# A second convolution tile moved to VectorE while the projections run, and its diagonals loaded from DRAM

## The reference

```
z = h @ w_in                      # 1024 -> 22 tiles of 128 columns
cv_v, cv_g, lr_x, lr_y, q, k, v, g_lr, og = split(z)
u = cv_v * sigmoid(cv_g)
u = causal_dw_conv(u, conv_dw_w, conv_dw_b)    # 31 taps, 256 channels
u = silu(layer_norm(u, conv_ln_g, conv_ln_b))
r = rg_lru(causal_dw_conv(lr_x, ...), ...) * gelu(lr_y)
o = rms_norm(gla_chunked(q, k, v, lg), gla_norm_g) * silu(og)
mixed = concatenate([u, r, o]);  return mixed @ w_out
```

## Time and profile before

| | us |
|---|---|
| median of 3 runs | 2758.78 (2758.22 to 2760.03) |
| profiled execution, its own time | 2758.25 |
| span of the profiled execution | 2756.4 |
| TensorE busy | 2672.3 (97%) |
| VectorE busy | 1997.5 (72%) |
| ScalarE busy | 1463.9 (53%) |
| GpSimd busy | 190.8 (7%) |

### The profile page before, as it was taken

How to read it: one execution, slowest core, us unless ns; L and a number is a source line. 1 busy time by engine, 2 the same in 40 slices (tenths; PEclk the granted TensorE clock), 3 DMA queues, 4 the chain that set the end, 5 groups by cost and what they waited for, 6 DMA issues and landing times.

```text
span 2756.4 us, 46105 instructions
## 1 busy us (share of the span) xinstructions
PE 2672.3 (97%) x15974; PEld 2315.9 (84%) x15974; DVE 1997.5 (72%) x2965; ACT 1463.9 (53%) x2276; POOL 190.8 (7%) x70
## 2 busy tenths in 40 slices
PE   5999899999999989999999999999999999999999
PEld 3866778887999867788899987999877888899987
DVE  7855699998997556743899847998465753699954
ACT  3353589986554246742655525555246753555532
POOL 1431133330000000000000000000000000000000
PEclk9999899999999999999999999999999999999999
DMA  7740599992322231123233232232232123223222
GB/s 288 280 137 32 204 344 412 412 391 100 102 100 92 99 145 62 50 80 109 93 105 107 92 107 92 94 106 92 99 131 83 53 69 115 100 93 107 91 100 99
DMA packets 95470, 376.63 MB, mean 137 GB/s; under 512 B 10800, under 2 KB 11072, under 8 KB 93120
## 3 DMA queue, kind: packets, MB, share of 16 engines
q1 hardware_dynamic: 89584, 348.69, 35.3%
q0 software_dynamic: 4320, 15.73, 1.4%
q10 hardware_dynamic: 1456, 10.74, 1.0%
HBM read 363.59 MB, written 15.73 MB: 138 GB/s over the span
## 4 chain that ended last, share of the span: by engine, by line
PE 84%; DVE 6%; issue 4%; ACT 4%; DMA 1%; POOL 0%; ACTq 0%; DVEq 0%; SPq 0%; POOLq 0%
PE pb L1442 15%; PE pb L1443 15%; PE pb L1444 15%; PE pb L1887 10%; PE pb L1888 10%; PE pb L1889 10%; PE pb L2071 1%; PE pb L2103 1%; PE pb L2027 1%; PE pb L1521 1%; ACT SP L1324 1%; DVE hid L2818 1%; PE pb L1726 1%; PE pb L2080 1%; DVE SP L2970 0%
## 5 line engine op out<-in xcount | busy, mean ns | idle before, releaser
L1887 PE MATMUL pb<-bl,g_wh 128*128 128x256 f32 x2464 | 702.1, 285 | 11.0 <-DVE bl L2729 6.9
L1888 PE MATMUL pb<-bh,g_wl 128*128 128x256 f32 x2464 | 698.3, 283 | 0.0
L1889 PE MATMUL pb<-bh,g_wh 128*128 128x256 f32 x2464 | 698.2, 283 | 0.0
L1887 PEld LDWEIGHTS pb<-bl,g_wh 128*128 128x128 f32 x2464 | 473.6, 192 | 15.9 <-issue 9.7
L1888 PEld LDWEIGHTS pb<-bh,g_wl 128*128 128x128 f32 x2464 | 473.7, 192 | 1.6 <-issue 1.4
L1889 PEld LDWEIGHTS pb<-bh,g_wh 128*128 128x128 f32 x2464 | 473.7, 192 | 0.0
L2768 DVE TENSOR_TENSOR w_lo<-raw,w_hi 128x1024 fp32r<-128x1024 f32 x164 | 200.3, 1222 | 202.0 <-ACT w_hi L694 201.2
L1442 PE MATMUL pb<-hl,w_hi 128*128 128x512 f32 x720 | 299.9, 416 | 20.6 <-DVE hl L2231 9.9
L694 ACT ACTIVATE w_hi<-raw 128x1024 fp32r<-128x1024 f32 x194 | 204.3, 1057 | 187.9 <-PE pb L1444 174.0
L1443 PE MATMUL pb<-hh,w_lo 128*128 128x512 f32 x720 | 283.3, 393 | 0.0
L1444 PE MATMUL pb<-hh,w_hi 128*128 128x512 f32 x720 | 283.2, 393 | 0.0
(11 more groups left out here) (476 smaller groups left out, 5456.2 us busy)
## 6 DMA issues: line engine op xcount, KB each, us to landing
raw<-in_wstream SPq DMA_DIRECT2D x220, 512.0 KB, 3.3
m_raw<-in_moe_stream SPq DMA_DIRECT2D x96, 512.0 KB, 8.3
g_own<-in_gu_stream SPq DMA_DIRECT2D x44, 768.0 KB, 4.1
raw<-in_gu_stream SPq DMA_DIRECT2D x44, 768.0 KB, 4.2
m_first<-in_moe_stream SPq DMA_DIRECT2D x48, 512.0 KB, 6.7
hf<-in_moe_stream SPq DMA_DIRECT2D x48, 512.0 KB, 6.4
ada_ring<-in_ada SPq DMA_DIRECT2D x8, 2048.0 KB
g_own<-in_gu_stream SPq DMA_DIRECT2D x44, 256.0 KB, 3.1
```

Of the source, the lines that this page charges most:

```text
L1887: pe.matmul(o, lh, rl, start=first and k == 0, stop=False, skip_group_check=True)
L1888: pe.matmul(o, ll, rh, start=False, stop=False, skip_group_check=True)
L1889: m = pe.matmul(o, lh, rh, start=False, stop=k == 3, skip_group_check=True)
```

## The change

- Tile 1 has 5 taps on TensorE instead of 13. The other 26 are on VectorE, and they stand before `route_add`, in groups of 3, 6, 5, 6 and 6.
- Between these groups VectorE makes the low halves of chunks 18 to 21, which GpSimd made.
- GpSimd no longer builds diagonals. They come from a new DRAM input `conv_diag`, 36 matrices of 128x128, with one transfer on SyncE's queue after the loads of pairs 8 and 9, when VectorE is done with `ada_ring`, whose memory they take.
- TensorE does the 5 taps and the identity matmul before the heads, in one go. No taps stand between heads. The two ones matmuls stand before `head_rms(3)`.
- ScalarE's `conv_evac(1)` stands before the first head's square.

```diff
-PE_TAPS = (CONV_K, 13)
-DIAG = tuple((t, k) for t in range(NU) for k in range(0, PE_TAPS[t], TAPS))
+PE_TAPS = (CONV_K, 5)
+N_DIAG = sum(PE_TAPS)
+EARLY = (3, 6, 5, 6, 6)
...
-            stream((ADA - ADA1) // ADA_EACH, C_WOUT // 2 + 1)
+            n_ada = (ADA - ADA1) // ADA_EACH
+            stream(n_ada, n_ada + 2)
+            sp.wait_ge(ada_used, n_ada)
+            sp.dma_start(diag[:, 0:N_DIAG, :], conv_diag).then_inc(diag_ready, 16)
+            stream(n_ada + 2, C_WOUT // 2 + 1)
...
             low(j0, 0)
-            pool.wait_ge(con_in, 16)
-            pool.wait_ge(vec_in, 48)
-            pool.wait_ge(ada_used, (ADA - ADA1) // ADA_EACH)
             low(j0, 1)
-            for i, (j, s) in enumerate(((j0 + 1, 0), (j0 + 1, 1), (j0 + 2, 0))):
-                diagonals(i, i + 1)
-                low(j, s)
-            diagonals(3, len(DIAG))
-            low(j0 + 2, 1)
...
+            conv_evac(1)
             head_square(0)
...
             head_root(GH - 1)
-            conv_evac(1)
...
             pe.wait_ge(conv_out, 1)
-            conv(1, 0, TAPS)
+            conv(1, 0, PE_TAPS[1])
+            pe.wait_ge(u_ready, 3)
+            pe.matmul(pb[7][:], ident, hidf[:], start=False, stop=True, skip_group_check=True).then_inc(conv_mm, 1)
...
                 m.then_inc(gla_mm, 1)
-                conv(1, TAPS + h, TAPS + h + 1)
                 if h >= 1:
                     head_rms(h - 1)
-            conv(1, TAPS + GH, PE_TAPS[1])
-            head_rms(GH - 1)
-            pe.wait_ge(u_ready, 3)
-            pe.matmul(pb[7][:], ident, hidf[:], start=False, stop=True, skip_group_check=True).then_inc(conv_mm, 1)
-
+            pe.wait_ge(o_root, 1)
             for t in range(NU):
                 pe.wait_ge(conv_out, t + 1)
                 m = pe.matmul(pb[0][:], ones, z[:, Z_CG + t, :], start=t == 0, stop=t == NU - 1)
             m.then_inc(ln_mm, 1)
+            head_rms(GH - 1)
             pe.wait_ge(o_ready, GH)
...
+            def taps(first, n):
+
+                for k in range(first, first + n):
+                    u, w = u_pad[:, 1, k:k + T], V("conv_w", CONV_K + k)
+                    if k == PE_TAPS[1]:
+                        ins = dve.tensor_scalar(hidf[:], u, w, None, ALU.mult)
+                    else:
+                        ins = dve.scalar_tensor_tensor(hidf[:], u, w, hidf[:], ALU.mult, ALU.add)
+                    if k == CONV_K - 1:
+                        ins.then_inc(u_ready, 1)
+                    else:
+                        step(ins)
+
+            dve.wait_ge(u_ready, 2)
+            k = PE_TAPS[1]
+            for i, n in enumerate(EARLY):
+                taps(k, n)
+                k += n
+                if i < 4:
+                    j, half = C_WOUT // 2 - 2 + i // 2, i % 2
+                    dve.wait_ge(w_lod, 2 * j + half)
+                    dve.wait_ge(w_hid, 2 * j + half + 1)
+                    dve.tensor_tensor(w_lo[half][:], raw[half][:], w_hi[half][:].bitcast(F32), ALU.subtract).then_inc(w_lod, 1)
             dve.wait_ge(consts_or_ov_c_mm, 1)
             dve.tensor_tensor(route_add[:], pb[5][:, 0:20], V("router_b", 0, 20), ALU.add).then_inc(mod_ready, 1)
```

More of the change, by code:

```diff
@@ L189, with build @@
     ("ident", P), ("ones", P), ("pairs", P), ("upto", P), ("iota", P), ("chunk_mask", T)])
-def build(nc, xT, cond, ada, wstream, gu_stream, vecs, lvecs, const, masks, lru_gates, gla_gate, moe_stream, na_bias, sw_bias, h_rows, y_rows, out):
+def build(nc, xT, cond, conv_diag, ada, wstream, gu_stream, vecs, lvecs, const, masks, lru_gates, gla_gate, moe_stream, na_bias, sw_bias, h_rows, y_rows, out):
     ctx = ExitStack()
@@ L643, in put @@
                                         ).then_inc(y_out, 16)
[L645 to L650, removed]
             j0 = C_WOUT // 2 - 3
@@ L1518, in conv @@
                 for k in range(first, end):
-                    if k % TAPS == 0 or k == first:
-                        pe.wait_ge(diag_ready, -(-CONV_K // TAPS) * t + k // TAPS + 1)
                     m = pe.matmul(pb[7][:], diag[:, CONV_K * t + k, :], u_pad[:, t, k:k + T], start=k == 0, stop=k == CONV_K - 1,
@@ L1526, in _ @@
             pe.wait_ge(u_ready, 2)
+            pe.wait_ge(diag_ready, 16)
             conv(0, 0, TAPS_1)
@@ L2375, in _ @@
             dve.tensor_tensor(mt[:, 0:NR, :], mt[:, 0:NR, :], z[:, Z_LY:Z_LY + NR, :], ALU.mult).then_inc(lru_ready, 1)
[L2377 to L2386, removed]
             dve.wait_ge(lru_ready, 2)
@@ L3238, in lay_out @@
     gg = head_pad(a["gla_w_gate"][0], DK, GH, 64).reshape(16, 2, P)
-    return dict(cond=a["c"], ada=ada_c.transpose(3, 0, 2, 1).reshape(P, ADA, D),
+    taps = np.zeros((P, N_DIAG, P), f)
+    for t in range(NU):
+        for k in range(PE_TAPS[t]):
+            taps[np.arange(P), CONV_K * t + k, np.arange(P)] = a["conv_dw_w"][0][k, P * t:P * t + P]
+    return dict(cond=a["c"], conv_diag=taps, ada=ada_c.transpose(3, 0, 2, 1).reshape(P, ADA, D),
                 xT=a["x"][0].T.reshape(KD, P, T).transpose(1, 0, 2), wstream=ws, gu_stream=gu_stream, vecs=vecs, lvecs=lv, const=con,
```

## The result

The changed kernel takes 2768.34 us in the median of 8 runs (2760.3 to 2774.98), the kernel before 2759.06 beside it (2757.43 to 2760.03). The ratio is 1.0033, 95% interval 1.0023 to 1.0042: slower by 0.3%. The forecast was 2756, with a range to 2759.4. The runs also spread over 15 us, where these of before spread over 3.

The account below looks back on a forecast made before the run. TensorE was taken as the bound, with a dependent chain through head_rms(3) to the first output tile. Fewer matmuls (-4.3) and a clock drop (+1.6) sum to -2.7 us, giving 2756 us, range 2753.3 to 2759.4.

Parts of the forecast that it names:

- the units: TensorE's mixer stage: of eight 0.86 us matmuls removed, five leave the path ahead of head_rms(3), gaining 4.3 us.
- dependent latency of 3.96 us: Before the output projection: time from the start of head_rms(3) to the first output tile, taken as unchanged.
- the hole: TensorE ahead of the first output tile: idle for 2.9 us after head_rms(3)'s matmul.
- VectorE, GpSimd, SP at no cost: Early taps and splits, GpSimd's removed work, diagonal transfer: each 0 us; upper bounds 1 us (VectorE, SP), 2.1 us (GpSimd).
- the hole's drop: After TensorE's idle time before the output projection: granted clock falls to half, costing 1.6 us, bounds 0 to 1.7.
- TensorE, the mixer stage: Step counting matmuls ahead of head_rms(3): 13 units become 8, gaining 4.3 us, with 2.9 us idle before the output tile.
- Rival D: Projection stage: dearer taps make VectorE the bound and the LRU convolution late; slower, about 2766 us; chance 0.07.
- Rival A: Idle hole before the output projection: the clock holds, so the full 4.3 us is won, 2754.5 us; chance 0.26.

Follow-up runs that it names:

- E4: Changed kernel with TensorE's mixer stage and ScalarE's order put back as before (13 taps on TensorE), the rest of the change kept: 2760.71 us, ratio 1.0004.
- E1: The changed kernel run again without any edit, 5 runs: median 2769.98 us, ratio 1.0041 to the kernel before.
- E11: The kernel of E8 once more, unedited, beside E9 on the same chip: median 2760.29 us, ratio 1.0002 to the kernel before.
- E2: Changed kernel with three dummy 128x512 fp32 matmuls after head_rms(3), in TensorE's idle hole: median 2764.07 us, ratio 1.0021 to the kernel before.
- E3: Changed kernel with the two ones matmuls moved behind head_rms(3): median 2765.52 us in 12 runs, ratio 1.001 to the kernel before.
- E12: The kernel of E6 once more, unedited, 5 runs: median 2770.55 us, ratio 1.0042 to the kernel before.
- E6: Kernel before, with the four taps that stood between the heads moved ahead of the first head: median 2768.99 us, ratio 1.0032.
- E5: Changed kernel with one dummy 128x512 fp32 matmul after each of the four heads: median 2762.37 us, ratio 1.0008 to the kernel before.
- E10: E9 with three unused ScalarE copies ahead of the last head's root, to lengthen TensorE's idle hole: median 2760.28 us.
- E9: E8 with taps and sums of squares spread through the heads, and each head's root before the next square: median 2756.2 us, ratio 0.999.
- E8: Changed kernel with nine tile 1 taps on TensorE, one after each head, ones matmuls last, conv_evac(1) after the last root: 2758.8 us, ratio 0.9993.

## Why the prediction was wrong

**Right: the units.** Five units left the path ahead of head_rms(3), and it started 4.4 us earlier after the 1.26 us of lateness that the profile has from elsewhere. The dependent latency of 3.96 us held to the hundredth (238.19 - 234.23), and the hole to 0.04 us.

**Right: VectorE, GpSimd, SP at no cost.** VectorE was done with the taps at 165.1 us (forecast 165.9), no new wait of TensorE arose from 140 to 210, the diagonals landed at about 149 (forecast: before 150), and E4 gives the whole package 1.0004 (0.9995 to 1.0013).

**Right in kind, mis-sized: the hole's drop.** I took 1.6 us, with 1.7 as the upper bound, from one drop of 3.4 us. In the first profile it was 6.8 us at half rate. From the output tile to the next ones matmuls (L1620) it took 7.70 us, where before took 4.92 (241.34 to 246.26): 2.8 us lost. In E1's profile it was 3.4 us, and 1.5 lost. The same holes far behind differ as much: the one up to about 1006, on which I built the term, is followed by 3.4 us at half rate in the trace of before and by 6.8 in the first profile, and another near 1705 likewise. That is enough to explain why the first profile, 0.4 us ahead of before at L1620, ends 2.0 us behind it.

**Wrong: the missing term.** The step that failed is "TensorE, the mixer stage", where the taps between the heads are units of 0.86 us that "leave the path", and all other matmuls keep their time. I looked for the clock only where TensorE idles. But the taps between the heads had been keeping the clock up, or bringing it back soon (E11). Without them it mostly falls while TensorE is busy, and stays down: the heads and what follows run at half rate for 20 to 27 us (E1, E2, E3, E12). The sum lacks a term for this, worth 8 to 12 us in the runs that have it. On E1's profile the sum is: output tile at 238.19 - 241.34 = -3.15 us as in the first profile, +12.3 for the drop in the heads, together 250.50 - 241.34 = +9.2; the drop after the hole and what comes later make it +11.7 at the end of the span. The median of the changed kernel moved by 9.3.

The windows of before gave no warning, since their busy share is 1.00, with or without taps. The timeline did: between two taps there is 3.4 us of matmuls of 64 and 128 columns, and after the change 7 us of them. The Trainium skill, TensorE: Matmul & The Clock Gate, section "What's actually happening", says that the ratio is set by how busy TensorE has recently been. If that is read as the busy share of the profile, the traces don't agree: E1's windows show 4.00 of 4.00 us busy at a clock of 0.50.

Rival D had the sign, by another mechanism (VectorE late), which didn't happen. Rival A's case, no drop in the hole or the heads, is what the four lower runs of E3 look like by their time and clock; none of them was profiled, and E3's hole is shorter.

**Not settled:** why the first profile of the changed kernel kept its clock through the heads, as E6's did, and why two of eleven runs of E5 lost it in spite of a dummy after each head; the same program does both. E1, E3 and E5 lost it within 0.3 us of the end of the first head, after hardly more small matmuls than before has between two taps. That the placement of the drops relative to the matmuls differs from run to run is argued, not shown. Nor is it known what makes the wait near 81 us 1.0 or 2.0 us long. The three profiles without the early stage of the change start the second tile's taps at 209.54 to 209.78, the eleven with it at 209.72 to 212.47. Six of the eleven have the longer wait, and three of these (E3, E4, E10) a drop of 3.4 us behind it. As kernels that are equal up to the heads are among the early and the late ones, and before was profiled only once, this can't be put down to the change; E4's interval bounds it.

## What to carry to other kernels

Before dense matmuls are taken from between small ones, look at what is left between them: if they were what kept TensorE's clock up, they cost less than their time, and removing them can cost more than it gives. Weave dense and small matmuls rather than bunch them: E12 and E9 are 14 us apart, and TensorE's work differs by four taps (3.4 us). The order alone, with the same work, is worth 8.4 and 11.9 us (before against E6 and E12). And run such a change several times, since the one execution that is profiled can be the one without the drop.

## What was not expected of the hardware

- The granted clock fell to half while TensorE was busy in every window (E1, E12), where only matmuls of 64 to 128 columns had run for 3.6 us (E1) and 5.7 us (E12), and stayed there for 20 to 27 us.
- Once it is down, the stretch keeps it down: the heads then take 7.7 us each with their sum of squares (225.41 to 233.11) where they took 4.3, and the 96x96 by 512-column matmul of each head doesn't bring it back. With a tap ahead of that matmul it came back after 3.4 us, twice, in E11; in E5, with a dummy in the tap's place, only at the second such pair (239.3).
- The clock fell behind an idle hole of 2.0 us in three profiles (E3, E4 and E10, near 81 us) and not behind one of 2.0 to 2.2 us in three others (the first profile, E1, E8). So the shortest hole with a drop is well under the 2.9 us that I took as near it.
- By their times, ten of 11 runs of the bunched kernel had the loss, none of 11 of the woven one, and eight of 12 of E3. For a kernel like E3 a median of three can miss it.
